# Gate, up and down products of a decoder step with every weight tile used as two tiles of 64 rows

## What is computed

```python
def _merge_ffn(x, o_heads, y_ssm, mg, w_attn_out, w_glu, w_out, g_ffn, w_gate, w_up, w_down):
    ya = o_heads.reshape(B, T, Q_COLS) @ w_attn_out
    yg = jax.nn.gelu(y_ssm) @ w_glu
    yb = yg[..., :D_MODEL] * jax.nn.sigmoid(yg[..., D_MODEL:])
    m = jax.nn.sigmoid(mg[:, :, 0]) * ya + jax.nn.sigmoid(mg[:, :, 1]) * yb
    x = x + m @ w_out
    h = _rmsnorm(x, g_ffn)
    return x + (jax.nn.silu(h @ w_gate) * (h @ w_up)) @ w_down
```

## Time and profile before

| | |
|---|---|
| median of 3 runs | 2205.86 us (2203.68 to 2211.8) |
| profiled execution, from its first to its last instruction (span) | 2206.9 us |
| TensorE busy, matmul records | 2091.7 us (95%), 15964 |
| VectorE busy | 1070.8 us (49%) |
| ScalarE busy | 806.2 us (37%) |
| DMA | 364.75 MB, mean 165 GB/s |
| mean granted TensorE clock | 0.974 of full speed |

### The profile page before, as it was taken

How to read it: one execution, slowest core, us unless ns; L and a number is a source line. 1 busy time by engine, 2 the same in 40 slices (tenths; PEclk the granted TensorE clock), 3 DMA queues, 4 the chain that set the end, 5 groups by cost and what they waited for, 6 DMA issues and landing times.

```text
span 2206.9 us, 39164 instructions
## 1 busy us (share of the span) xinstructions
PE 2091.7 (95%) x15964; PEld 1952.5 (88%) x15964; DVE 1070.8 (49%) x1725; ACT 806.2 (37%) x1164; POOL 112.5 (5%) x168
## 2 busy tenths in 40 slices
PE   8999898898899788899999999999999999999997
PEld 6999787787898455589999999999999999999996
DVE  4343487853465344464564444444444444444443
ACT  5222232243244355574433433323332333233344
POOL 1000011000000121200001000000000000000011
PEclk9999899999897899999999999999999999999999
DMA  7645543443455888855655455455445554555443
GB/s 179 200 133 152 134 129 102 112 117 94 119 164 212 323 326 324 304 178 163 197 179 152 134 153 152 137 162 154 145 134 154 161 152 134 144 160 151 146 132 114
DMA packets 552965, 364.75 MB, mean 165 GB/s; under 512 B 64737, under 2 KB 528050, under 8 KB 552018
## 3 DMA queue, kind: packets, MB, share of 16 engines
q1 hardware_dynamic: 471042, 314.00, 46.3%
q10 hardware_dynamic: 80096, 41.25, 7.0%
q0 software_dynamic: 1712, 7.97, 1.0%
HBM read 345.45 MB, written 23.63 MB: 167 GB/s over the span
## 4 chain that ended last, share of the span: by engine, by line
PE 55%; issue 7%; SPq 1%; DMA 1%; DVE 1%; ACT 1%; POOL 1%; POOLq 0%; DVEq 0%; ACTq 0%
PE bank L279 54%; SPq L1277 1%; SPq L1278 1%; POOL ysT L1726 0%; DMA arena<-in_cache_kv_dram 0%; DMA xT<-out_dram 0%; DVE w_lo L255 0%; PE bank L1859 0%; PE bank L1834 0%; ACT w_hi L250 0%; PE bank L2075 0%; POOL arena L1736 0%; DVE rstd L2589 0%; PE bank L1793 0%; ACT xT L2328 0%
## 5 line engine op out<-in xcount | busy, mean ns | idle before, releaser
L279 PE MATMUL bank<-hx,w_hi 128*128 128x320 f32 x3072 | 676.3, 309 | 1.5 <-DVE w_lo L255 1.5
L255 DVE TENSOR_TENSOR w_lo<-w_raw,w_hi 128x2048 fp32r<-128x2048 f32 (+2 forms) x222 | 463.9, 2089 | 348.3 <-ACT w_hi L250 348.2
L279 PE MATMUL bank<-act,w_hi 128*128 128x320 f32 x2432 | 537.0, 310 | 3.2 <-DVE w_lo L255 2.4
L279 PEld LDWEIGHTS bank<-hx,w_hi 128*128 128x128 f32 x3072 | 513.5, 188 | 2.0 <-issue 1.8
L250 ACT CAST w_hi<-w_raw 128x2048 fp32r<-128x2048 f32 (+2 forms) x222 | 385.6, 1737 | 319.7 <-PE bank L279 317.7
L279 PE MATMUL bank<-hx,w_lo 128*128 128x320 f32 x1536 | 474.6, 309 | 0.0
L279 PEld LDWEIGHTS bank<-act,w_hi 128*128 128x128 f32 x2432 | 405.6, 188 | 4.6 <-DVE w_lo L255 3.1
L279 PE MATMUL bank<-act,w_lo 128*128 128x320 f32 x1216 | 375.8, 309 | 0.0
L279 PEld LDWEIGHTS bank<-hx,w_lo 128*128 128x128 f32 x1536 | 288.4, 188 | 0.0
L662 PE MATMUL bank<-actr,half_hi 128*128 128x320 f32 x1024 | 241.4, 325 | 19.3 <-DVE half_lo L633 19.2
L279 PEld LDWEIGHTS bank<-act,w_lo 128*128 128x128 f32 x1216 | 228.3, 188 | 0.0
(11 more groups left out here) (396 smaller groups left out, 1846.3 us busy)
## 6 DMA issues: line engine op xcount, KB each, us to landing
arena<-in_cache_kv_dram SPq DMA_DIRECT2D x120, 512.0 KB, 6.6
w_raw<-in_w_gate_dram SPq DMA_DIRECT2D x44, 1024.0 KB, 5.2
w_raw<-in_w_up_dram SPq DMA_DIRECT2D x44, 1024.0 KB, 5.2
w_raw<-in_w_down_dram SPq DMA_DIRECT2D x64, 704.0 KB, 4.6
half_raw<-in_w_in_dram ACTq DMA_DIRECT2D x64, 512.0 KB, 4.1
w_raw<-in_w_in_dram SPq DMA_DIRECT2D x20, 1024.0 KB, 5.1
w_raw<-in_w_glu_dram SPq DMA_DIRECT2D x32, 512.0 KB, 4.9
w_raw<-in_w_out_dram SPq DMA_DIRECT2D x16, 1024.0 KB, 5.8
```

The lines of the kernel that those rows point to most:

```text
L255: nc.vector.tensor_tensor(w_lo[s][:, 0:job.kt * job.width], raw[s][:, 0:job.kt * job.width], w_hi[s][:, 0:job.kt * job.width].bitcast(F32) ...
L279: mm = pe.matmul(bank[:, 0:NT], w[s][:, at:at + P], x[:, kk, :], start=first and k == 0 and m == 0, stop=final and k == job.kt - 1 and m == 2)
```

## The change

Gate, up and down jobs get `halves=True`. Each product of 128 rows becomes two of 64 rows, the upper and the lower half of the same weight tile and of the same activations, issued by turns, and each half sums in a bank of its own: `PS[2 * s + r]` for half r of slot s. The reader adds the two banks. The output projection `job_out` is not halved, but moves to `PS[0]` and `PS[2]` (`apart=2`), since a slot's banks are now two. The banks 4 to 7 are used as before.

```diff
         class Job:
-            def __init__(self, n, kt, columns, dmas=1, joined=False, wide=1):
+            def __init__(self, n, kt, columns, dmas=1, joined=False, wide=1, halves=False, apart=1):
...
+                self.halves, self.apart = halves, 2 if halves else apart
...
-                bank = PS[0 if job.joined else own if own is not None else s * job.wide + side]
+                bank = PS[0 if job.joined else own if own is not None else s * job.wide * job.apart + side]
...
-                        mm = pe.matmul(bank[:, 0:NT], w[s][:, at:at + P], x[:, kk, :],
-                                       start=first and k == 0 and m == 0, stop=final and k == job.kt - 1 and m == 2)
+                        if job.halves:
+                            for r in range(2):
+                                rows = slice(64 * r, 64 * (r + 1))
+                                mm = pe.matmul(PS[2 * s + r][:, 0:NT], w[s][rows, at:at + P], x[rows, kk, :],
+                                               start=k == 0 and m == 0, stop=k == job.kt - 1 and m == 2)
+                        else:
+                            mm = pe.matmul(bank[:, 0:NT], w[s][:, at:at + P], x[:, kk, :],
+                                           start=first and k == 0 and m == 0, stop=final and k == job.kt - 1 and m == 2)
...
-                            V.tensor_tensor(tg, PS[0][:, 0:NT], rstd[:, :], ALU.mult).then_inc(S("bank_free0"), 1)
+                            link(V.tensor_copy(tg, PS[0][:, 0:NT]))
+                            link(V.tensor_tensor(tg, tg, PS[1][:, 0:NT], ALU.add))
+                            V.tensor_tensor(tg, tg, rstd[:, :], ALU.mult).then_inc(S("bank_free0"), 1)
...
-                            V.tensor_tensor(tmp, PS[1][:, 0:NT], rstd[:, :], ALU.mult).then_inc(S("bank_free1"), 1)
+                            link(V.tensor_copy(tmp, PS[2][:, 0:NT]))
+                            link(V.tensor_tensor(tmp, tmp, PS[3][:, 0:NT], ALU.add))
+                            V.tensor_tensor(tmp, tmp, rstd[:, :], ALU.mult).then_inc(S("bank_free1"), 1)
...
-                        V.tensor_tensor(xr[:, t, :], xr[:, t, :], PS[s][:, 0:NT], ALU.add).then_inc(S(f"bank_free{s}"), 1)
+                        link(V.tensor_tensor(xr[:, t, :], xr[:, t, :], PS[2 * s][:, 0:NT], ALU.add))
+                        V.tensor_tensor(xr[:, t, :], xr[:, t, :], PS[2 * s + 1][:, 0:NT], ALU.add).then_inc(S(f"bank_free{s}"), 1)
```

More of the change, by code:

```diff
@@ L348, in build @@
         job_ao = Job(4, 8, lambda i, s: [w_ao[:, bass.ds(i * 512 + s * 256, 256)]], wide=2)
-        job_out = Job(8, KT, plain(w_out))
+        job_out = Job(8, KT, plain(w_out), apart=2)
         job_ffn, job_down = [], []
         for c in range(FC):
-            job_ffn.append(Job(FK, KT, lambda i, s, c=c: [(w_gate, w_up)[s][:, bass.ds(i * P + c * FK * P, P)]]))
-            job_down.append(Job(8, FK, lambda i, s, c=c: [w_down[c * FK * P:(c + 1) * FK * P, bass.ds(i * 256 + s * P, P)]]))
+            job_ffn.append(Job(FK, KT, lambda i, s, c=c: [(w_gate, w_up)[s][:, bass.ds(i * P + c * FK * P, P)]], halves=True))
+            job_down.append(Job(8, FK, lambda i, s, c=c: [w_down[c * FK * P:(c + 1) * FK * P, bass.ds(i * 256 + s * P, P)]], halves=True))
         with ExitStack() as alias:
@@ L2575, in during_out @@
                         dve.wait_ge(S("x_back"), 16)
-                    V.tensor_tensor(xr[:, t, :], xr[:, t, :], PS[s][:, 0:NT], ALU.add).then_inc(S(f"bank_free{s}"), 1)
+                    V.tensor_tensor(xr[:, t, :], xr[:, t, :], PS[2 * s][:, 0:NT], ALU.add).then_inc(S(f"bank_free{s}"), 1)
                     if t:
```

## The result

| | before | after |
|---|---|---|
| median of six runs, us (lowest to highest) | 2207.16 (2203.68 to 2211.80) | 2216.99 (2211.67 to 2220.86) |
| ratio of the times, 95% interval | | 1.0046 (1.0031 to 1.0061) |
| span of the profiled execution, us | 2206.9 | 2209.9 |

The account below looks back on a forecast made before the run. TensorE's product count times pitch was taken as the bound (6336 x 0.1467 = 929 us). Terms 0 + 0.8 + 1.2 + 4.0 + 2.0 + 1.1 + 0.5 = +9.6 us gave 2216 us; range 2166 to 2300, the mechanism's own 2206 to 2230.

Parts of the forecast that it names:

- The pair, 147 ns, term 0: Gate, up and down products: two halves together cost one full product, 147 ns, adding 0; argued partly from float32 rows; chance 0.60.
- Ten mode switches, +0.8: Ten changes between 128-row and 64-row products on TensorE, 0.08 us each, +0.8 us in all.
- rows 5: Trace of short full-height and 64-row product runs, giving the switch cost and up to 13 ns extra a pair.
- Up tiles, 0.03 on 40, +1.2: Up tiles: 1.04 us of new VectorE work nearly fills 1.06 us of slack; 0.03 us on 40 tiles, +1.2 us.
- Second tile of each down chunk, 4 x 1.0: Second down tile in each of four chunks: slack only 0.06 us, so each stalls by 1.0 us, +4.0 us.
- Stalls that exist, +2.0: Three existing TensorE waits for w_lo lengthen: +1.0 at the FFN's start, +0.5 each for two in the last chunk.
- Last chunk, +1.1: Last chunk's down tiles: no slack, so every second tile of the first six waits, 2 x 0.54, +1.1 us.
- the circle: Tile's last product, VectorE's bank read, ScalarE's rounding (w_hi), VectorE's remainder (w_lo), then that slot's next tile; extra work costs beyond slack.
- The last sum, +0.5: End of the last chunk: the last sum of all comes 0.5 us later.
- Faster by the 13 ns: Rival: the 13 ns a product beyond streaming vanish when halves run together; 2170 us, or 2194 with half; chance 0.15.
- Halves in turn: Rival: the halves' loads or products cannot run at once; +464 us (2680) or +929 us (3145); chance 0.12.
- Waits in all, "some 12 us": Sign: TensorE's waits for w_lo total some 12 us, where 3.9 stood before.

Follow-up runs that it names:

- One bank read: The changed kernel with VectorE reading only the first bank, as before the change, so the lower halves are missing from the result: 2210.44 us, ratio 1.0012.
- Rounding a tile ahead: The changed kernel with ScalarE rounding the tile after next before its part of the current tile's reading: 2209.60 us, ratio to before 1.0010.
- the adds alone: Full products of 128 rows as before, but VectorE's copy and adds from two banks as in the changed kernel: 2222.63 us, ratio 1.0055.
- 256 columns: The kernel before, with gate, up and down products of 256 of the 320 tokens as moving columns: 2057.36 us.
- three by three: The changed kernel issuing three products of the upper rows, then three of the lower, by turns: 2222.74 us.
- upper half: The changed kernel with only the upper half's 6336 products of 64 rows, VectorE still adding two banks: 2948.74 us.
- rounding ahead in the kernel before: The kernel before, with ScalarE rounding the tile after next before its part of the current tile's reading: 2205.04 us, ratio 0.9983.
- 64 columns of weights: The kernel before, with gate, up and down products using the first 64 of 128 weight columns: 2202.60 us.

## Why the prediction was right, and where it was off

The forecast of 2216 us met 2217, and the likeliest case was the one that happened. That the mechanism holds is shown by the pair's pitch and by the two runs that take the change apart; that the sum came within a microsecond is in part luck, since it left out the clock and had some smaller terms too large or too small. By its own steps:

- **The pair, 147 ns, term 0: right.** One bank read costs 1.4 us in all for 6336 pairs. The gap that the prediction named, float32 rows standing for float32r, didn't matter. Of the bounds, the +13 ns of the short run belonged to its slow first pair: in its trace the first step is 173 ns and the next two are 109.
- **Ten mode switches, +0.8: half of what they cost.** One bank read holds all of them and comes to +1.4. A group of transposes in the last chunk costs 0.33 more than before, two switches of 0.17. The prediction took from rows 5 only the first start behind a switch (0.19 us for 0.11); in the same trace the second is late as well, 0.14 us for 0.11 into the full products and 0.17 for 0.11 back.
- **Up tiles, 0.03 on 40, +1.2: too much.** The three later gate/up stretches grew by 0.5 together, so some 0.65 in four. The slack of 1.06 us was almost exactly used up: w_lo of one is ready at 1502.18, the hundredth in which the tile before begins its last pair.
- **Second tile of each down chunk, 4 x 1.0: right.** The stretches grew by 1.01 to 1.02. Rounding a tile ahead takes nearly all of it away (77.58), which shows that it is the way through ScalarE's order.
- **Stalls that exist, +2.0: right in size.** Start to start, the first grew by 0.83 and the two in the last chunk by 0.52 each.
- **Last chunk, +1.1: right, but not the whole.** Of the stretch's +4.3, the second tile has 1.0, the old stalls 1.0, the circle 0.9 and the switches 1.0. The rest is 0.1 us at each of the three groups of transposes, which the run of the adds alone shows too (6.16 us for the tile with its group, where before has 6.07).
- **The last sum, +0.5: right for its wait** (2.54 for 2.02).
- **The step that was missing: what a longer wait does to the clock.** The prediction priced each stall at its own length. After the 2.37 us at the second gate tile TensorE ran at the lower level, +1.5 us, and so it did in each of the four other profiles with this wait at 2.4 to 2.6 us. At the end the transposes took +1.2; whether that belongs to the longer wait is less sure, since other runs show it behind a wait of 2.02 as well. Together 2.7 us, more than the difference between the predicted 9.6 and the 11.9 of the profiled execution; the end gave 0.8 back (from the transposes to the end of the span 11.8 us for 12.5).
- **The rivals.** Faster by the 13 ns: refuted by the pitch, and the runs with 256 and with 64 columns show why. The 13 ns are there for a half as for the whole, so a neighbour doesn't remove them. The Trainium skill's "TensorE: Matmul & The Clock Gate", section The mechanism, which has a load overlap a running product only in other row groups, would have made the change a gain; the 6336 pairs at the full products' pitch speak against it. The same section also lets a load go ahead into a background weight buffer; the rows fit that, since full products keep 147 ns with a load for each. Halves in turn: it exists, but only where the order leaves one half alone for long (2991 us) or where both use the same rows (3129).
- **Waits in all, "some 12 us": 9.2 in the profile**, since a late tile's wait is shown shorter than its start-to-start delay (0.75 for 0.91) and the up tiles didn't wait.

By medians the loss is 10 us and in the profiled executions 11.9; the interval, 6.8 to 13.5 us, holds both, so it doesn't decide whether the end's 1.2 us belong to the change.

## What to carry to other kernels

Splitting a full-height product into two halves of 64 rows bought nothing here, where the full one already streamed at its pitch: the pair costs the same, and the sum of the second bank is pure extra. Price such extra work by the slack of the circle it stands in (here 1.06, 0.06 and 0 us), not by the engine's busy share; 117.6 us more of VectorE's busy time cost 10. Look then at what an idle stretch is followed by: a stall that grew from 1.5 to 2.4 us was followed by a fall of the clock that cost 1.5 us more. And where an engine reads a bank and also makes the next tile's weights, let the weights go first.

## What the runs showed of the hardware

- Products on different halves of the array run beside each other even when the program gives three of one and then three of the other, 147 ns a pair (2222.74 us). On the same half they go one by one, 147 ns each, with one bank or two.
- A float32r product of 320 columns takes 147 ns at 2.4 GHz, of 256 columns 120: one column a cycle and 13 ns. With 64 columns of weights for 128 it is 147 still. At 1.2 GHz it is 267, with nothing added. A float32 transpose of 128 columns takes 109 and 213 ns.
- At the second gate tile the clock fell in all five profiles with a wait of 2.4 to 2.6 us (after, adds alone, rounding ahead, three by three, upper half), and in none of the four with 1.3 to 1.6 us (before, one bank read, rounding ahead in the kernel before, 64 columns of weights); yet with 256 columns it stayed through a wait of 2.8 us there, and fell behind one of 2.1 us in the last chunk. At the end the twelve transposes took 2.76 to 2.82 us behind each wait of 2.54 (seven profiles), but behind 2.02 they took 1.53 twice, and 1.97, 2.37 and 2.82 with 64 columns of weights, with rounding ahead in the kernel before and with 256 columns, and 2.82 in the two runs that ended with single products on the upper rows and one bank read. So a longer gap makes the fall likelier, and its length alone doesn't decide it.
- With one product a step on 64 rows the clock fell at or behind gaps of only 1.33 and 1.20 us (up to 2.3 us behind a gap's end). With nothing else between them such products then stayed at the lower level, 267 ns each, for over 1570 us; with no gap they kept 147 for 660 us, and 12672 products on the same 64 rows kept it too. The level rose again only around groups of 12 full-height transposes in the last chunk, at six of the eight groups that found it low, from just before the group's end to 1.1 us behind it, and the half-height products that followed kept it until the next gap. That rests on one execution each of four kernels, and whether such a stream alone would ever bring the clock back was not seen.
- The Trainium skill's "TensorE: Matmul & The Clock Gate" gives, in the section Wait — 56ns, not 53.3ns?, a fixed 2.5 ns a matmul at 2.4 GHz and none at 1.2. The kind agrees with these runs, and so does the size for the float32 transposes (2 ns); for the float32r products it is 13 ns, and the measurement decides.
